# First modulation of a hybrid decoder block, loaded and summed in groups of feature tiles

## The reference, cut to what matters

```
c_act = silu(c)
mod = c_act @ ada_w[0] + ada_b[0]                # (1, 6144)
sh_m, sc_m, gt_m, sh_f, sc_f, gt_f = split(mod, 6)
h = rms_norm(x, norm_g[0, 0]) * (1 + sc_m) + sh_m
y = hybrid_mixer(h, w_in[0], ...)                # proj = h @ w_in, then attention, SSD, gates
x = x + gt_m * rms_norm(y, norm_g[0, 1])
h = rms_norm(x, norm_g[0, 2]) * (1 + sc_f) + sh_f
x = x + gt_f * rms_norm(squared_relu_mlp(h, w_up[0], w_down[0]), norm_g[0, 3])
```

## Time and profile before

| what | value |
|---|---|
| median of 3 runs | 2376.72 us (2376.52 to 2377.8) |
| the profiled execution's own time | 2377.7 us |
| its span | 2375.6 us |
| TensorE matmuls busy | 2308.2 us, 97% |
| VectorE busy | 1344.5 us, 57% |
| ScalarE busy | 747.5 us, 31% |
| GpSimd busy | 961.0 us, 40% |

### The profile page before, as it was taken

The page is one execution under the profiler, slowest core; times in us unless marked ns, Lnnn a source line. Parts: engine busy times, 40 slices in busy tenths (PEclk is TensorE's granted clock), DMA queues, the critical chain, the costliest instruction groups (busy, mean ns, idle before and its releaser), DMA issues.

```text
span 2375.6 us, 31731 instructions
## 1 busy us (share of the span) xinstructions
PE 2308.2 (97%) x11882; PEld 1904.5 (80%) x11882; DVE 1344.5 (57%) x1997; ACT 747.5 (31%) x1360; POOL 961.0 (40%) x628
## 2 busy tenths in 40 slices
PE   5999999999999999999999999999999999999997
PEld 5877888875558998989887888899788888888886
DVE  5379999996567167776858544425422322322325
ACT  5252210115552345545375101035412112112113
POOL 2312332327763453736545343356233233223322
PEclk9999999999999999999999999999999999999999
DMA  7101442325560113131313543334111111111113
GB/s 278 54 18 71 173 155 89 132 78 187 170 198 24 50 54 133 59 132 46 137 54 139 183 141 136 106 114 158 66 54 38 51 53 44 45 53 52 36 35 80
DMA packets 144875, 230.28 MB, mean 97 GB/s; under 512 B 7972, under 2 KB 111748, under 8 KB 143876
## 3 DMA queue, kind: packets, MB, share of 16 engines
q1 hardware_dynamic: 120080, 166.11, 21.2%
q10 hardware_dynamic: 23684, 59.06, 6.5%
q0 software_dynamic: 1008, 3.67, 0.9%
HBM read 176.39 MB, written 52.43 MB: 96 GB/s over the span
## 4 chain that ended last, share of the span: by engine, by line
PE 89%; DVE 5%; issue 2%; ACT 1%; SPq 1%; DMA 1%; DVEq 0%; ACTq 0%
PE ps L659 87%; DVE score L1788 2%; SPq L390 1%; DVE probT L1871 1%; PE ps L1008 1%; PE ps L904 1%; PE ps L941 1%; DMA x_tm<-in_x_dram 1%; PE ps L709 0%; DMA gate_d<-last_spill 0%; ACT decay L1540 0%; DVE a_lo L1924 0%; DVE prob L1854 0%; DVE acc L2015 0%; DVE score L1790 0%
## 5 line engine op out<-in xcount | busy, mean ns | idle before, releaser
L659 PE MATMUL ps<-a_hi,w_hi 128*128 128x512 f32 (+1 forms) x1744 | 683.1, 392 | 1.9 <-DVE a_lo L1924 1.2
L659 PE MATMUL ps<-a_lo,w_hi 128*128 128x512 f32 (+1 forms) x1744 | 679.1, 389 | 0.0
L587 POOL CAST w_hi<-raw 128x2048 fp32r<-128x2048 f32 x90 | 174.5, 1939 | 1159.5 <-issue 854.0
L659 PE MATMUL ps<-a_hi,w_lo 128*128 128x512 f32 (+1 forms) x1744 | 548.1, 389 | 0.0
L591 POOL TENSOR_TENSOR w_lo<-raw,w_hi 128x512 fp32r<-128x512 f32 (+1 forms) x360 | 523.8, 1487 | 7.2
L2085 DVE TENSOR_TENSOR x_tm<-x_tm,ps 128x1024 f32<-128x1024 f32 x120 | 146.6, 1221 | 453.7 <-PE ps L659 453.1
L659 PEld LDWEIGHTS ps<-a_hi,w_hi 128*128 128x128 f32 (+1 forms) x1744 | 327.1, 188 | 71.1 <-DVE a_lo L1924 1.9
L659 PEld LDWEIGHTS ps<-a_hi,w_lo 128*128 128x128 f32 (+1 forms) x1744 | 327.0, 188 | 69.0
L659 PEld LDWEIGHTS ps<-a_lo,w_hi 128*128 128x128 f32 (+1 forms) x1744 | 327.2, 188 | 67.4 <-issue 0.2
L659 PE MATMUL ps<-w_hi,a_hi 128*128 128x256 f32 x832 | 242.8, 292 | 3.8 <-DVE a_lo L1924 2.7
L659 PE MATMUL ps<-w_lo,a_hi 128*128 128x256 f32 x832 | 236.4, 284 | 0.0
(11 more groups left out here) (264 smaller groups left out, 3055.4 us busy)
## 6 DMA issues: line engine op xcount, KB each, us to landing
raw<-in_w_in_dram SPq DMA_DIRECT2D x35, 1024.0 KB, 5.0
ada_raw<-in_ada_w_dram SPq DMA_DIRECT2D x16, 1024.0 KB, 8.7
raw<-in_w_up_dram SPq DMA_DIRECT2D x16, 1024.0 KB, 5.4
raw<-in_w_down_dram SPq DMA_DIRECT2D x16, 1024.0 KB, 4.7
gates<-gate_d SPq DMA_DIRECT2D x12, 1024.0 KB, 4.9
act_raw<-acts_d ACTq DMA_DIRECT2D x20, 512.0 KB, 5.6
acts_d<-decay ACTq DMA_DIRECT2D x16, 512.0 KB, 3.5
raw<-in_w_o_ssd_dram SPq DMA_DIRECT2D x8, 1024.0 KB, 7.4
```

What stands on the lines that cost most here:

```text
L587: nc.gpsimd.tensor_copy(hi, src).then_inc(hi_made, 1)
L659: return nc.tensor.matmul(o, a, b, start=start, stop=stop)
```

## The change

The 2048 columns are now cut into four groups g of two feature tiles: columns g * 256 to g * 256 + 255 of the shift and the same of the scale. A group is loaded in four pieces (two halves of k, shift and scale), so there are 16 loads of 512 KB with rows of 1 KB. The order of the queue is: tokens 0 to 3, group 0, group 1, key-value weights, group 2, tokens 4 to 7, group 3, small weights. VectorE makes 32 products of 512 columns, half a group at a time, and between them the gains of the group before (`mod_gains`) and the splits that are ready by the program's order. TensorE sums four columns a group (`mod_columns`), ahead of the even steps of the projection; the 60 unread transposes are gone; the turns of the first half are spread over the steps, and five turns of the second half stand ahead of its first step, three ahead of the next ones. ScalarE evacuates tiles 0 to 3 before the squares of tokens 4 to 7, tiles 4 and 5 behind them.

```diff
-        ada0 = place("ada0", [P, KT, 2 * D], F32, ACT_AT)
+        ada0 = place("ada0", [P, 2, 4, KT, WC], F32, ACT_AT)
...
-        IDLE_TURNS = 60
-        FIRST_TURN = (4, 5, 6, 7, 2, 3) + (4, 5, 6, 7) * 2 + (4, 5)
+        MOD_BANK = (1, 3, 2, 3)
+        FIRST_TURN = (4, 5, 6, 7)
...
-            for k in range(KT):
-                if k < KT - 1:
-                    sp.dma_start(ada0[:, k, :], ada_w[0, k * P:(k + 1) * P, 0:2 * D]).then_inc(ada_in[k], 16)
-            for half in range(2):
-                c = slice(half * D, half * D + D)
-                sp.dma_start(ada0[:, KT - 1, c], ada_w[0, D - P:D, c]).then_inc(ada_last if half else ada_in[KT - 1], 16)
+            def load_first_ada(g):
+                for half in range(2):
+                    rows_k = slice(half * 4 * P, half * 4 * P + 4 * P)
+                    for part in range(2):
+                        c0 = part * D + g * WC
+                        sp.dma_start(ada0[:, part, g, 4 * half:4 * half + 4, :],
+                                     ada_w[0, rows_k, c0:c0 + WC].rearrange("(k p) c -> p k c", p=P)).then_inc(ada_in[2 * g + half], 16)
+            load_first_ada(0)
+            load_first_ada(1)
             load(0, cols(w, C_KV))
+            load_first_ada(2)
             load_tokens(range(4, NT))
+            load_first_ada(3)
...
-            norm_turn(0, range(6), banks=FIRST_TURN)
-            for i in range(IDLE_TURNS):
-                nc.tensor.transpose(ps[:, 1, (i % 4) * P:(i % 4 + 1) * P], x_tm[:, i % 4, 0:P], ident[:, :])
-            for m in range(2 * KT):
-                if m % KT == 0:
-                    pe.wait_ge(mod0_summed, m // KT + 1)
-                last = mm(ps[:, 0, m:m + 1], mod_sum[:, m * P:(m + 1) * P], ones[:, 0:1], start=True, stop=True)
-            last.then_inc(c_ready, 1)
+            def mod_columns(g):
+                pe.wait_ge(mod0_summed, g + 1)
+                for m in range(4):
+                    part, k = divmod(m, 2)
+                    col = part * KT + 2 * g + k
+                    last = mm(ps[:, MOD_BANK[g], col:col + 1], mod_sum[:, (4 * g + m) * P:(4 * g + m + 1) * P], ones[:, 0:1],
+                              start=True, stop=True)
+                last.then_inc(c_ready, 1)
+            mod_columns(0)
+            norm_turn(0, range(4), banks=FIRST_TURN)
...
             for k in range(KT):
-                norm_turn(0, (6 + k,), banks=FIRST_TURN)
+                if k % 2 == 0 and k < KT - 1:
+                    if k // 2 + 1 < 4:
+                        mod_columns(k // 2 + 1)
+                norm_turn(0, (4 + k,) if k < 4 else (), banks=FIRST_TURN)
                 pe.wait_ge(w_split[0], k * LO_PARTS // KT + 1)
                 kv_step(k, range(4))
-            norm_turn(0, (14, 15), banks=FIRST_TURN)
             for k in range(KT):
+                norm_turn(0, range(KT, KT + 5) if k == 0 else (KT + 4 + k,) if k < 4 else (), banks=FIRST_TURN)
                 last = kv_step(k, range(4, NT))
...
-                    if i == 0 and j == 0:
-                        act.wait_ge(gain_ready, 1)
                     g = i // KT
+                    if g == 0 and j == 0 and k % 2 == 0:
+                        act.wait_ge(gain_ready, k // 2 + 1)
...
+            norm_evac(0, 0, range(4), banks=FIRST_TURN)
             token_squares(range(4, NT))
-            norm_evac(0, 0, range(2), banks=FIRST_TURN)
+            norm_evac(0, 0, range(4, 6), banks=FIRST_TURN)
...
+            def mod_products(g, half):
+                dve.wait_ge(ada_in[2 * g + half], 32)
+                o = mod_sum[:, g * 2 * WC:(g + 1) * 2 * WC].rearrange("p (a c) -> p a c", a=2)
+                for k in range(4 * half, 4 * half + 4):
+                    if k == 0:
+                        V.link(ve.tensor_scalar(o, ada0[:, :, g, k, :], c_act[:, k:k + 1], None, ALU.mult))
+                    else:
+                        ins = ve.scalar_tensor_tensor(o, ada0[:, :, g, k, :], c_act[:, k:k + 1], o, ALU.mult, ALU.add)
+                        if k < KT - 1:
+                            V.link(ins)
+                        else:
+                            ins.then_inc(mod0_summed, 1)
+            def mod_gains(g):
+                k0 = 2 * g
+                shift, scale = (ps[:, MOD_BANK[g], part * KT + k0:part * KT + k0 + 2] for part in range(2))
+                scaled = ps[:, MOD_BANK[g], 2 * KT + k0:2 * KT + k0 + 2]
+                dve.wait_ge(c_ready, 2 + g)
+                V.add(ve.tensor_tensor(mod[:, k0:k0 + 2], shift, vec_a[:, k0:k0 + 2], ALU.add))
+                V.link(ve.tensor_tensor(scaled, scale, vec_a[:, 56 + k0:58 + k0], ALU.mult))
+                ve.tensor_tensor(gain[:, k0:k0 + 2], scaled, gain[:, k0:k0 + 2], ALU.add).then_inc(gain_ready, 1)
...
-            mod_product(0)
+            mod_products(0, 0)
             dve.wait_ge(squares, 1)
             ve.tensor_scalar(stat[:, 0:4], stat[:, 0:4], 1.0 / D, EPS, ALU.mult, ALU.add).then_inc(vars_ready, 1)
             dve.wait_ge(roots, 1)
             ve.reciprocal(stat[:, NT:NT + 4], stat[:, 0:4]).then_inc(vars_ready, 1)
+            mod_products(0, 1)
+            for g in range(1, 4):
+                mod_products(g, 0)
+                mod_gains(g - 1)
+                if g == 3:
+                    dve.wait_ge(squares, 2)
+                    ve.tensor_scalar(stat[:, 4:NT], stat[:, 4:NT], 1.0 / D, EPS, ALU.mult, ALU.add).then_inc(vars_ready, 1)
+                mod_products(g, 1)
+                norm_split(0, (2 * g - 2, 2 * g - 1))
+            mod_gains(3)
             dve.wait_ge(roots, 2)
             V.link(ve.reciprocal(stat[:, NT + 4:2 * NT], stat[:, 4:NT]))
             for t in range(4, NT):
                 ve.tensor_scalar(x_tm[:, t, :], x_tm[:, t, :], stat[:, NT + t:NT + t + 1], None, ALU.mult).then_inc(normed, 1)
                 if t % 2:
-                    norm_split(0, (t // 2,))
-            norm_split(0, range(4, 2 * KT))
+                    norm_split(0, (4 + t // 2,))
+            norm_split(0, range(KT, 2 * KT))
```

More of the change, by code:

```diff
@@ L274, in hybrid_block @@
         c_ready = sem("c_ready")
-        ada_last = sem("ada_last")
         gain_ready = sem("gain_ready")
@@ L1266, in _ @@
                 nc.scalar.activation(x_tm[:, t, :], x_tm[:, t, :], ACT.Copy, scale=stat[:, NT + t:NT + t + 1]).then_inc(normed, 1)
+            norm_evac(0, 0, range(4), banks=FIRST_TURN)
             token_squares(range(4, NT))
-            norm_evac(0, 0, range(2), banks=FIRST_TURN)
+            norm_evac(0, 0, range(4, 6), banks=FIRST_TURN)
             act.wait_ge(vars_ready, 3)
             nc.scalar.activation(stat[:, 4:NT], stat[:, 4:NT], ACT.Sqrt).then_inc(roots, 1)
-            norm_evac(0, 0, range(2, 2 * KT), banks=FIRST_TURN)
+            norm_evac(0, 0, range(6, 2 * KT), banks=FIRST_TURN)
             act.wait_ge(w_used[0], 1)
```

## The result

The changed kernel took 2381.49 us (median of 17 runs, 2379.65 to 2383.43), the kernel before 2377.69 us (17 runs, 2375.55 to 2378.71): a ratio of 1.0017, 95% interval [1.0011, 1.0023]. The forecast was 2381.0 us from a median of 2376.72, a ratio of 1.0018. So the total came out as forecast. The way to it did not, and the agreement is luck: the point on which the whole sum was made moved by 1.80 us instead of 4.2, and about 2 us more arose behind it, where the forecast had put nothing, half of them in one place 1200 us later. The profiled execution took 2380.59 us around a span of 2378.7.

What follows compares the result with a forecast made beforehand. VectorE's products bound the modulation, and everything later waits for TensorE. First-half end 1.1, restart 1.8 and three moved turns 1.3 sum to +4.2 us on 2376.72: 2380.9, rounded to 2381.0; range 2372.5 to 2386.0.

Steps and rivals of the forecast that it cites:

- the point: Start of the next block's first matmul on TensorE, after the first projection: 73.14 before, forecast 77.3, +4.2 us.
- the whole rest: Everything behind the first projection waits for TensorE, so it shifts by exactly what the point shifts by.
- several us: Modulation loads: group 3 lands at 39.5, several us before VectorE asks for it at about 44.5.
- cover of 1.2 us: ScalarE's squares of tokens 4 to 7 end at 46.3; VectorE asks at 47.5, behind group 3's first half.
- VectorE's term: VectorE's chain in the first half: split 7 done at 52.4 undisturbed, 60.3 with 7.9 us lost to GpSimd.
- The meeting with GpSimd: GpSimd's weight splits delay VectorE's full stretch: 5.7 us for the key-value weights, 2.2 for the small ones, sum 7.9.
- rival B: VectorE and GpSimd exclude each other for full durations, 10 us instead of 7.9: +6.3 in all, 2383.0 us; chance 0.45.
- TensorE's end for this half about 1.1: First half of the projection on TensorE ends at 62.0 instead of 60.92, costing about 1.1 us.
- Restart 1.8: TensorE between steps 7 and 8: tile 8's turn, evacuation and split take 2.65 instead of 0.87, costing 1.8 us.
- Three turns behind 1.3: Three turns of 0.44 moved behind the start of step 8 on TensorE cost 1.3 us.
- The transposes at nothing: TensorE's 60 unread transposes are removed at no cost, since nothing waits for them.
- They did not hold the clock either: The 60 unread transposes did not keep TensorE's clock up: granted 0.55 in 36 to 38, during the column sums.

Runs made afterwards that it cites:

- a_smallsplit: The changed kernel with GpSimd splitting only one eighth of the key-value weights, the rest left out: 2381.55 us for 2378.02 before, ratio 1.0013.
- a_turns: The changed kernel with the turns of tiles 8 to 11 ahead of step 7 instead of behind it: 2380.19 us for 2378.02 before, ratio 1.0010.
- b_noidle: The kernel before without its 60 unread transposes, nothing else changed: 2380.05 us, ratio 1.0008 to the kernel before.
- a_idle: The changed kernel with the 60 unread transposes put back behind its first four turns: 2380.19 us for 2378.16 before, ratio 1.0008.
- b_idle128: The kernel before with 68 more unread transposes ahead of its first turn, 128 in all: 2379.60 us for 2377.73 before, ratio 1.0009.
- b_early4: Kernel before with k = 1 product, evacuations and splits of tiles 0-3 earlier, turns 8-13 paired ahead of steps 5-7, 36 unread transposes: 2375.20 us, ratio 0.9988.

## Why the prediction was right, and where it was not

**The number** was right by luck, by two errors that cancel: the point moved 1.80 for 4.2 (2.4 too much), and about 2 us arose behind it, where "the whole rest" was to be "shifted by what 73.14 is shifted by".

**What bounds.** VectorE's queue from 18.6 on, without gaps: right (18.48). That groups 2 and 3 wait for no transfer: right, but their cover was 1.5 us at group 3, as a_smallsplit shows, not "several us". The products of the first half group ended at 17.92 instead of 16.2, so the variances came 1.0 later; the forecast's "one for one" did not hold, since ScalarE loads a table from 16.77 to 18.05 before the roots in any case. The squares of tokens 4 to 7, priced as cover of 1.2 us, ended at 45.1, and VectorE asked at 46.15: 1.0.

**VectorE's term**, "split 7 done at 60.3", was mis-sized: 57.5. The meeting with GpSimd was 5.6 for the key-value weights (forecast 5.7) and 1.4 for the small ones (2.2), 7.0 for 7.9. The other 1.9 us are small parts taken too long, each used three or four times: a second half takes 3.02 (3.15), gains 0.35 (0.5), a pair of splits 1.66 (1.82), because unlinked instructions overlap a little at their ends (the row that starts at 24.70 lasts 3.10, and the next one starts at 27.72). Parts read from a row's length and not from the distance of two starts count that overlap twice.

The rule of the Trainium skill, page "SBUF — State Buffer", of a port pair held exclusively, would have given rival B's 10 us and a point at +6.3. Measured were 7.0, so rival B did not come true; but GpSimd's cast took 2.39 us here against 1.90 in the earlier trace rows and its four subtractions 6.09 against 5.03, so both sides lost time to the other, as it is when, by that page of the Trainium skill, whichever comes second waits.

**TensorE's terms.** "TensorE's end for this half about 1.1" was wrong in sign: -1.58. Nearly all of it is VectorE's term, since steps 6 and 7 waited for their splits (0.59 and 0.73 us). Two others were too large as well and are hidden by these waits but for some 0.3: the four columns of group 3 took 1.05 us, not 1.8, and steps 4 and 5 took 2.9 us for both (24 matmuls from 51.59) where the forecast had 4.2 (54.9 to 59.1), all of it with 1.00 granted in 50 to 54. "Restart 1.8" was about right in size (2.06), and a_turns shows that the order of the turns makes most of it. "Three turns behind 1.3" was right: 1.32.

**The transposes at nothing** is the step that failed: "the 60 idle transposes go: nothing waits for them". Nothing waits for their result, and at their own place taking them out moved the point by 0.24 (b_noidle). But they are TensorE instructions, and taking them out moved the later loads of its instructions into a stretch full of transfers. b_noidle has this part alone (+1.8 beyond its point, of the 3.8 of the whole change, uncertain by 2; 1.2 of it stands in its trace between the first and the fourth write), a_idle is without it, and b_idle128 brings it with transposes added instead of removed.

The forecast's "They did not hold the clock either" was wrong for the first eight columns, which took 1.95 us in the kernel before; without the transposes all 32 records took 6.99 (b_noidle).

**The transfers.** The Trainium skill's page "DMA: Bandwidth & Descriptors" would have put group 3 some 2 us later than the forecast's 39.5, and its first half did land at 41.2 in the changed kernel. But the cause is another. The two loads of the very first half group landed at 13.0 and 15.0, where the forecast had 13.3 for both, and from there to group 3 it took 26.2 us, as forecast (13.3 to 39.5); at 16 to 28 us these loads moved 348 GB/s, above the 320 of that estimate. The rate taken from one landing of the earlier trace rows was right, the first landing was 1.7 us off, and it happened not to matter.

## What to carry to other kernels

Cutting a vector stage into smaller groups so that the next engine can start early gains only if the vector engine is not itself the bound; look first at what else works beside it, because a split of weights on GpSimd cost VectorE 5.6 us here; and look at the transfers next, for with most of that split left out VectorE waited for them, and only 1.1 us was won. When instructions are added to or taken from TensorE's program, even unread ones, compare the places where many transfers meet with the places of the instruction loads, before any shift of 2 us in a kernel of this length is put down to the edit itself. And fill the gap at a restart by moving ready turns ahead of the step that waits: that alone gave 1.1 us, and an earlier product and earlier evacuations with it gave the 2.8 us of b_early4.

## What had not been expected of the hardware

TensorE's instructions arrive as single packets of 16 KB, 72 in the changed kernel and 73 before, each about 1 us of one DMA engine (0.9 to 1.5 for nine in ten) and a median of 127 matmuls with their weight loads apart. Taking out 60 transposes moved one of them from 1304 to 1322 us, and a kernel with 128 has them where a kernel with none has them. With a load amid the stores ScalarE's idle time ahead of its third write was 4.4 to 5.1 us in eight kernels; without, 2.5 to 2.7 in six.
